# Two transformer blocks on one core: last units completed by bank, the Sqrt's table loaded before the squares, the second next split after the norm, first two units interleaved

## Chip, core and metric

The kernel runs on one core of a Trainium2 chip. The metric is the device time of one execution in microseconds (us); lower is better. Engines: TensorE (PE, with PEld for its weight loads), VectorE (DVE), ScalarE (ACT), GpSimd (POOL) and SyncE (SP), which here only issues DMAs.

## What is computed

256 tokens of width 1024, in fp32, pass through a first block (FFN, token mixer, FFN, with an RMS norm ahead of each and one behind) and a second of two layers (attention with convolution, then an expert layer). Every sublayer has the same frame:

```python
h = modulate(rms_norm(x, g), shift, scale)        # mean of squares over 1024 channels, sqrt, divide
x = x + gate * sublayer(h)                        # shift, scale, gate from c by adaptive weights
# sublayers: 0.5 * swiglu(h, w_in, w_out)         (twice, 2816 hidden)
#            token_mixer(h) ... @ mix_w_out
#            merged(attention, conv) @ w_out      (per layer)
#            peer(h): experts, sum over 16384     (per layer)
return rms_norm(x, final_g)
```

## The kernel before

**Data.** Everything is held transposed: 128 channels on the partitions, 256 tokens along them, so x is eight tiles of 128x256 (`x_t`). Weights come as 864 *units* of 128x1024 fp32 (512 KB) in the order of their use, through `ring`, four slots filled by SP: the load for a slot waits until DVE has *taken* the unit before in it. For precision each unit is split: ACT copies it to `w_hi` (`hi`, line 393), DVE subtracts to get `w_lo` (`lo`, line 731), and PE computes a product of three parts: for each of eight tiles t `w_hi` with `h_hi` and with `h_lo`, then for each t `w_lo` with `h_hi`; 24 matmuls (`product`, lines 1452 to 1467). `w_hi` and `w_lo` have two buffers each, so unit u + 2 is split once unit u is done (semaphore `weights_used`, kept by PE): that is `step(u)` on ACT and DVE, and it is written there at the point where u is used. `first` and `shared` tell when an accumulation begins; `st` and `acc` are four PSUM banks each, and `acc_t` sees `acc` as eight tiles of 256, two to a bank.

**Two kinds of unit.** An *output* unit (`tile`) gives one 128x256 tile of a result and needs all eight tiles of h. A *row* unit (`accumulate`, `kmajor`) multiplies one tile of h and adds to all eight tiles of `acc_t`. A sublayer's last product is of row units: the FFN's down-projection (lines 1501 to 1503), `mix_w_out`, `w_out`. The experts' last product (`v_unit`, lines 1848 to 1865) has tokens on the partitions: 12 matmuls of 512 columns into four banks.

**Between two sublayers** stands one chain. After the last unit DVE adds `gate * acc_t` to `x_t` tile by tile (`add_to_x`, lines 839 to 844), ACT squares each tile as it is ready (line 418), PE sums the squares over the channels with a matrix of ones (line 1473), ACT takes the Sqrt (line 420), DVE the reciprocal (line 756), and then for each tile DVE multiplies (765), ACT adds the shift and rounds to `h_hi` (426), DVE gives `h_lo` (760), and PE's first unit waits for it tile by tile (`fresh`). Each stage ends in a barrier of all engines (`stage`). After the experts the sums have first to be copied to SBUF (ACT line 717, DVE line 1341, after the whole last unit) and transposed back by PE (line 1883).

**Order.** Each engine's program is written out by hand; nothing is rearranged. Within the last unit of a sum, `step` on ACT and DVE splits the *second* unit of the next sublayer before `add_to_x` and `squares`.

## Time and profile before

| | |
|---|---|
| median of three runs | 3363.89 us (3363.59 to 3364.19) |
| the profiled execution | 3363.27 us, span 3361.6 us |
| mean granted PE clock in it | 0.941 |
| PE busy | 3070.9 us, 91% of the span, 22464 matmuls |
| PE weight loads busy | 2828.1 us (84%) |
| DVE busy | 2346.1 us (70%) |
| ACT busy | 1358.5 us (40%) |
| ring loads | 864 of 512 KB, median 3.3 us from issue to landing |

A clock of 1.00 is PE's full one, 2.4 GHz, and 0.50 the other of its two levels, 1.2 GHz. Times in the timelines are from the start of the span. A row's bracket tells how long its engine had been idle and what ended that. Where a row stands for several instructions ("x8"), its length is from the first one's start to the last one's end.

### The profile page before, as it was taken

The page shows a single profiled execution, that of the slowest core. Times are in us where ns is not written, and L with a number is a line of the kernel's source. Part 1 is how long each engine was busy: PE and PEld are TensorE (multiplying, and loading weights), DVE is VectorE, ACT ScalarE, POOL GpSimd, SP SyncE. Part 2 cuts the span into 40 slices and gives each one's busy share as a digit, 9 for nine tenths or more (in the row PEclk, how much of TensorE's full clock was granted, in tenths as well). Part 3 has the DMA queues.
Part 4 walks back from the last instruction along what each step waited for, and adds up shares of the span by engine and source line. Part 5 has one row for each costly group of instructions (what it writes and reads, how often), then busy time and mean ns, then how long its engine had stood idle before and what let it go on. Part 6 is the DMA issues. An engine that isn't in the chain of part 4 may idle for free. (4 is left out here: it accounts for less than half of the span.)

```text
span 3361.6 us, 61755 instructions
## 1 busy us (share of the span) xinstructions
PE 3070.9 (91%) x22464; PEld 2828.1 (84%) x22464; DVE 2346.1 (70%) x3735; ACT 1358.5 (40%) x1960; POOL 185.4 (6%) x204
## 2 busy tenths in 40 slices
PE   3998988889989768999999999998799999999998
PEld 2998976779979668989998878797699899988887
...
DMA packets 149585, 547.98 MB, mean 163 GB/s; under 512 B 16608, under 2 KB 16736, under 8 KB 149088
## 3 DMA queue, kind: packets, MB, share of 16 engines
...
q8 instruction: 79, 1.29, 0.2%
q14 instruction: 34, 0.28, 0.0%
HBM read 545.29 MB, written 1.05 MB: 163 GB/s over the span
## 5 line engine op out<-in xcount | busy, mean ns | idle before, releaser
L731 DVE TENSOR_TENSOR w_lo<-ring,w_hi 128x1024 fp32r<-128x1024 f32 x864 | 1087.3, 1260 | 647.1 <-ACT w_hi L393 640.4
L393 ACT ACTIVATE w_hi<-ring 128x1024 fp32r<-128x1024 f32 x864 | 910.9, 1054 | 1124.5 <-PE st L1465 935.9
L1461 PE MATMUL st<-h_hi,w_hi 128*128 128x256 f32 x4064 | 1038.5, 292 | 42.8 <-DVE h_lo L760 26.7
L1462 PE MATMUL st<-h_lo,w_hi 128*128 128x256 f32 x4064 | 1016.1, 287 | 0.0
L1461 PEld LDWEIGHTS st<-h_hi,w_hi 128*128 128x128 f32 x4064 | 795.0, 196 | 62.6 <-issue 38.4
L1462 PEld LDWEIGHTS st<-h_lo,w_hi 128*128 128x128 f32 x4064 | 795.7, 196 | 1.0
L1465 PE MATMUL st<-h_hi,w_lo 128*128 128x256 f32 x4064 | 581.5, 286 | 23.1 <-DVE w_lo L731 22.8
L1465 PEld LDWEIGHTS st<-h_hi,w_lo 128*128 128x128 f32 x4064 | 532.3, 195 | 29.5 <-DVE w_lo L731 29.5
L1856 PE MATMUL acc<-w_hi,act_hi 128*128 128x512 f32 x1024 | 322.1, 396 | 3.8 <-DVE act_lo L1278 3.8
L1856 PE MATMUL acc<-w_hi,act_lo 128*128 128x512 f32 x1024 | 316.0, 390 | 0.0
L694 ACT ACTIVATE act_hi<-arena 128x256 fp32r (+1 forms) x256 | 106.5, 417 | 438.9 <-PE acc L1862 430.8
L1862 PE MATMUL acc<-w_lo,act_hi 128*128 128x512 f32 x1024 | 274.4, 390 | 0.0
L1856 PEld LDWEIGHTS acc<-w_hi,act_lo 128*128 128x128 f32 x1024 | 192.5, 188 | 40.8
L1862 PEld LDWEIGHTS acc<-w_lo,act_hi 128*128 128x128 f32 x1024 | 192.8, 188 | 40.1
L1856 PEld LDWEIGHTS acc<-w_hi,act_hi 128*128 128x128 f32 x1024 | 189.3, 190 | 40.2 <-issue 4.1
L1278 DVE TENSOR_TENSOR act_lo<-arena,act_hi 128x256 fp32r<-128x256 f32 x256 | 108.5, 425 | 128.7 <-ACT act_hi L694 127.2
L1829 PE MATMUL st<-extra 128*128 128x64 bf16 x3072 | 193.8, 246 | 4.0 <-DVE extra L1263 4.0
L1829 PEld LDWEIGHTS st<-extra 128*128 128x128 bf16 x3072 | 171.8, 123 | 24.3 <-issue 16.4
L1461 PE MATMUL acc<-h_hi,w_hi 128*128 128x256 f32 x416 | 115.9, 310 | 54.5 <-DVE h_lo L750 26.1
L1263 DVE TENSOR_TENSOR extra<-extra,k 128x1024 bf16<-128x1024 f32 (+1 forms) x128 | 155.9, 1218 | 0.0
L1258 DVE TENSOR_TENSOR extra<-extra 128x512 bf16<-128x512 bf16 x384 | 139.4, 418 | 0.0
L1461 PEld LDWEIGHTS acc<-h_hi,w_hi 128*128 128x128 f32 x416 | 89.5, 215 | 57.8 <-DVE h_lo L750 26.7
...
## 6 DMA issues: line engine op xcount, KB each, us to landing
ring<-weights SPq DMA_DIRECT2D x864, 512.0 KB, 3.3
...
```

Of the source, the lines that this page charges most:

```text
L393: nc_a.activation(w_hi[:, u % 2, :], ring[:, u % RING, :], ACT.Copy).then_inc(hi_ready, 1)
L694: nc_a.activation(act_hi[:, n % 2, :], src, ACT.Copy).then_inc(sem("gated_hi"), 1)
L731: v.tensor_tensor(w_lo[:, u % 2, :], ring[:, u % RING, :], w_hi[:, u % 2, :], ALU.subtract)\
L1258: ins = v.tensor_tensor(hot_r[b][k], hot_r[b][0], spread(gate_parts[:, k, :], g, i, HALF), ALU.mult)
L1263: v.tensor_tensor(hot_l[g % 2], keys_t[:, 0, tokens(g, i)].unsqueeze(2).to_broadcast([P, GROUP, NKEYS]), kc("iota").unsqueeze(1).to_broadc ...
L1278: v.tensor_tensor(act_lo[:, n % 2, :], src, act_hi[:, n % 2, :], ALU.subtract) .then_inc(sem("gated_lo"), 1)
L1461: mm(dst(t), w, hi_t(t), start=start, stop=False, skip_group_check=True)
L1462: mm(dst(t), w, lo_t(t), start=False, stop=False, skip_group_check=True)
L1465: ins = mm(dst(t), w_lo[:, u % 2, t * P:(t + 1) * P], hi_t(t), start=False, stop=last and (t == DT - 1 or not shared), skip_group_check=True)
L1829: ins = mm(st[:, 2 + g % 2, :].rearrange("p (n t) -> p n t", t=GROUP)[:, :, k], hot_l[g % 2][:, k, :], hot_r[g % 2][part_][:, k // 2, :, k ...
L1856: mm(acc[:, 2 * t + half, :], act_part[:, b, t * P:(t + 1) * P], w_hi[:, u % 2, 512 * half:512 * half + 512], start=False, stop=False, ski ...
L1862: ins = mm(acc[:, 2 * t + half, :], act_hi[:, b, t * P:(t + 1) * P], w_lo[:, u % 2, 512 * half:512 * half + 512], start=False, stop=last, ...
```

## The change

Four things, at every place where one sublayer ends and the next begins:

1. The last row unit of a sum (`finish`) does its three matmuls for a tile together, and signals after each bank of two tiles (`acc_bank`; the last by `weights_used`). `add_to_x` waits by bank. The experts' last unit (`last_v_unit`) likewise completes bank by bank (`y_bank`), and the four copies wait for their own bank. `finish` and `last_v_unit` wait for `w_lo` before their first matmul.
2. ACT runs a one-column Sqrt into `spare` before the squares, so the table of that function is loaded there.
3. `step` for the last unit is left out on ACT and DVE. The second next unit is split in `norm` (`second`): on ACT ahead of the norm's tiles, on DVE behind them. For ACT the last four bodies of the FFN loop are written out.
4. PE's first two units after a norm run side by side (`first_two`): for each tile both units' products with `w_hi` and the first unit's with `w_lo`, then the second unit's eight with `w_lo`. It waits for both units' `w_hi`. The first unit is signalled as done after the 40 matmuls.

```diff
@@ ScalarE @@
             def squares(n):
+                nc_a.activation(spare[:, :], kc("eps"), ACT.Sqrt)
                 for t in range(DT):
...
-            def norm(m, shift):
+            def norm(m, shift, second=None):
+                if second is not None:
+                    hi(second)
                 for t in range(DT):
                     eng.wait_ge(sem("nh"), DT * m + t + 1)
...
-                    step(base + 5 + 3 * j, i, per)
+                    if j < FT - 2:
+                        step(base + 5 + 3 * j, i, per)
...
-                with eng.Fori(0, (FT - 2) // 4) as i:
+                with eng.Fori(0, (FT - 6) // 4) as i:
                     for j in range(4):
                         body(1 + j, i, 12)
+                for j in range(FT - 5, FT - 1):
+                    body(j)
...
-            steps(U_MIXO, 8)
+            steps(U_MIXO, 7)
...
-                eng.wait_ge(used, nth(base + 2 * NKEYS - 1))
                 for half in range(2):
+                    eng.wait_ge(sem("y_bank"), 3 * l + 2 * half + 1)
                     nc_a.activation(y_tok[:, half, :], acc[:, half, :], ACT.Copy).then_inc(sem("y_act"), 1)
@@ VectorE @@
                 if b is not None:
                     lower(DT - 2)
                     lower(DT - 1)
+                if second is not None:
+                    lo(second)
...
-            def add_to_x(gate):
+            def add_to_x(gate, n, u):
                 for t in range(DT):
+                    if t < 6:
+                        eng.wait_ge(sem("acc_bank"), 3 * n + t // 2 + 1)
+                    else:
+                        eng.wait_ge(used, nth(u))
...
-                step(base + N_FFN - 1)
-                add_to_x(half_gate[:, 8 * f:8 * f + 8])
+                add_to_x(half_gate[:, 8 * f:8 * f + 8], (0, 2)[f], base + N_FFN - 1)
...
-                eng.wait_ge(used, nth(v_base + NKEYS - 1))
                 for half in range(2):
+                    if half == 0:
+                        eng.wait_ge(sem("y_bank"), 3 * l + 2)
+                    else:
+                        eng.wait_ge(used, nth(v_base + NKEYS - 1))
@@ TensorE @@
+            def finish(u, lhs_t, rhs_t, first=False):
+                eng.wait_ge(hi_ready, nth(u))
+                eng.wait_ge(taken, u + 1)
+                for t in range(DT):
+                    w = slice(t * P, (t + 1) * P)
+                    mm(acc_t[:, t, :], w_hi[:, u % 2, w], lhs_t, start=False, stop=False, skip_group_check=True)
+                    mm(acc_t[:, t, :], w_hi[:, u % 2, w], rhs_t, start=False, stop=False, skip_group_check=True)
+                    ins = mm(acc_t[:, t, :], w_lo[:, u % 2, w], lhs_t, start=False, stop=True, skip_group_check=True)
+                    if t % 2 == 1:
+                        ins.then_inc(used if t == DT - 1 else sem("acc_bank"), 1)
+
+            def first_two(u, dsts, fresh, one_bank):
+                eng.wait_ge(hi_ready, nth(u + 1))
+                eng.wait_ge(taken, u + 1)
+                for t in range(DT):
+                    w = slice(t * P, (t + 1) * P)
+                    eng.wait_ge(sem("norm_lo"), DT * fresh + t + 1)
+                    for k in range(2):
+                        mm(dsts[k], w_hi[:, (u + k) % 2, w], h_hi[:, t, :], start=t == 0 and not (one_bank and k),
+                           stop=False, skip_group_check=True)
+                        mm(dsts[k], w_hi[:, (u + k) % 2, w], h_lo[:, t, :], start=False, stop=False,
+                           skip_group_check=True)
+                    ins = mm(dsts[0], w_lo[:, u % 2, w], h_hi[:, t, :], start=False, stop=t == DT - 1,
+                             skip_group_check=True)
+                ins.then_inc(used, 1)
+                eng.wait_ge(taken, u + 2)
+                for t in range(DT):
+                    ins = mm(dsts[1], w_lo[:, (u + 1) % 2, t * P:(t + 1) * P], h_hi[:, t, :], start=False,
+                             stop=t == DT - 1, skip_group_check=True)
+                ins.then_inc(used, 1)
...
+                def last_v_unit():
+                    u, b = base + 2 * NKEYS - 1, (NKEYS - 1) % 2
+                    eng.wait_ge(sem("gated_lo"), n_key + NKEYS)
+                    eng.wait_ge(hi_ready, nth(u))
+                    eng.wait_ge(taken, u + 1)
+                    for half in range(2):
+                        for t in range(TT):
+                            cols = slice(512 * half, 512 * half + 512)
+                            for act_part, w in ((act_hi, w_hi), (act_lo, w_hi), (act_hi, w_lo)):
+                                ins = mm(acc[:, 2 * t + half, :], act_part[:, b, t * P:(t + 1) * P], w[:, u % 2, cols],
+                                         start=False, stop=w is w_lo, skip_group_check=True)
+                            ins.then_inc(used if (half, t) == (1, 1) else sem("y_bank"), 1)
```

The other calls of `norm`, `steps`, `add_to_x` and `kmajor` change in the same way; for the very first norm there is no second split, since both units are split before it.

ACT from the last steps of the first FFN's loop to the first steps of the mixer's projection, before:

```order
L393 ACTIVATE w_hi<-ring 128x1024 [waits weights_used]
L468 REGISTER_ALU
L468 COMPARE_AND_BRANCH
L418 ACTIVATE arena<-x_t 128x256 [waits x_tile] x8
L420 ACT_TABLE_LOAD
L420 ACTIVATE extra<-st,k 128x256 [waits sumsq]
L426 ACTIVATE h_hi<-arena,mod 128x256 [waits nh,stage_done]
L426 ACTIVATE h_hi<-arena,mod 128x256 [waits nh] x7
L393 ACTIVATE w_hi<-ring 128x1024 [waits weights_used,landed0]
L393 ACTIVATE w_hi<-ring 128x1024 [waits weights_used,landed1]
```

The same place on ACT in the changed kernel:

```order
L394 ACTIVATE w_hi<-ring 128x1024 [waits weights_used,landed1]
L457 ACTIVATE act_hi<-arena 128x256 [waits act]
L394 ACTIVATE w_hi<-ring 128x1024 [waits weights_used,landed2]
L417 ACT_TABLE_LOAD
L417 ACTIVATE spare<-k 128x1
L421 ACTIVATE arena<-x_t 128x256 [waits x_tile] x8
L423 ACTIVATE extra<-st,k 128x256 [waits sumsq]
L394 ACTIVATE w_hi<-ring 128x1024 [waits weights_used,landed3,stage_done]
L431 ACTIVATE h_hi<-arena,mod 128x256 [waits nh] x8
L394 ACTIVATE w_hi<-ring 128x1024 [waits weights_used,landed0]
L394 ACTIVATE w_hi<-ring 128x1024 [waits weights_used,landed1]
```

The last `w_hi` before the squares is gone, table and one-column Sqrt stand ahead of the squares, and that `w_hi` follows the norm's Sqrt.

DVE at the same exit, from the adaptive bias to the norm's reciprocal (`nscale` is the next norm's scale), before:

```order
L812 TENSOR_TENSOR mod<-mod,par 128x40 [waits ada_mod]
L898 TENSOR_SCALAR half_gate<-mod 128x8 [waits dve_chain]
L731 TENSOR_TENSOR w_lo<-ring,w_hi 128x1024 [waits w_hi_ready,dve_chain]
L842 SCALAR_TENSOR_TENSOR x_t<-acc,half_gate,x_t 128x256 x8
L815 SCALAR_TENSOR_TENSOR nscale<-mod,par 128x8
L815 SCALAR_TENSOR_TENSOR nscale<-mod,par 128x8 [waits dve_chain]
L756 RECIPROCAL extra<-extra 128x256 [waits dve_chain,std,stage_done]
```

The same place on DVE in the changed kernel:

```order
L823 TENSOR_TENSOR mod<-mod,par 128x40 [waits ada_mod]
L913 TENSOR_SCALAR half_gate<-mod 128x8 [waits dve_chain]
L857 SCALAR_TENSOR_TENSOR x_t<-acc,half_gate,x_t 128x256 [waits acc_bank,dve_chain]
L857 SCALAR_TENSOR_TENSOR x_t<-acc,half_gate,x_t 128x256 [waits acc_bank] x5
L857 SCALAR_TENSOR_TENSOR x_t<-acc,half_gate,x_t 128x256 [waits weights_used] x2
L826 SCALAR_TENSOR_TENSOR nscale<-mod,par 128x8
L826 SCALAR_TENSOR_TENSOR nscale<-mod,par 128x8 [waits dve_chain]
L765 RECIPROCAL extra<-extra 128x256 [waits dve_chain,std,stage_done]
```

The `w_lo` between the half gate and the adds has left, and the adds wait by bank.

PE from the squares' sums to the first tiles of the projection, before:

```order
L1473 MATMUL st<-arena,k 128x256 [waits sq] x8
L1461 MATMUL st<-h_hi,w_hi 128x256 [waits norm_lo,w_hi_ready,stage_done]
L1462 MATMUL st<-h_lo,w_hi 128x256
L1461 MATMUL st<-h_hi,w_hi 128x256 [waits norm_lo]
L1462 MATMUL st<-h_lo,w_hi 128x256
L1461 MATMUL st<-h_hi,w_hi 128x256 [waits norm_lo]
L1462 MATMUL st<-h_lo,w_hi 128x256
L1461 MATMUL st<-h_hi,w_hi 128x256 [waits norm_lo]
L1462 MATMUL st<-h_lo,w_hi 128x256
L1461 MATMUL st<-h_hi,w_hi 128x256 [waits norm_lo]
```

The same place on PE in the changed kernel:

```order
L1525 MATMUL st<-arena,k 128x256 [waits sq] x8
L1508 MATMUL st<-h_hi,w_hi 128x256 [waits w_taken,norm_lo,w_hi_ready,stage_done]
L1510 MATMUL st<-h_lo,w_hi 128x256
L1508 MATMUL st<-h_hi,w_hi 128x256
L1510 MATMUL st<-h_lo,w_hi 128x256
L1512 MATMUL st<-h_hi,w_lo 128x256
L1508 MATMUL st<-h_hi,w_hi 128x256 [waits norm_lo]
L1510 MATMUL st<-h_lo,w_hi 128x256
L1508 MATMUL st<-h_hi,w_hi 128x256
L1510 MATMUL st<-h_lo,w_hi 128x256
L1512 MATMUL st<-h_hi,w_lo 128x256
L1508 MATMUL st<-h_hi,w_hi 128x256 [waits norm_lo]
```

Each tile of the norm now releases five matmuls, four with `w_hi` of two units and one with `w_lo` of the first, where it released two.

## Rows read from the trace of the kernel before

**Rows 1.** The page's groups: ScalarE's copy of a unit's weights (busy us, mean ns | idle).
```profile
L393 ACT ACTIVATE w_hi<-ring 128x1024 fp32r<-128x1024 f32 x864 | 910.9, 1054 | 1124.5 <-PE st L1465 935.9
```

**Rows 2.** Timeline, exit of the first FFN (start us, us, engine, line, operation).
```profile
281.24 0.17 DVE L898 TENSOR_SCALAR half_gate<-mod 128x8 f32<-128x8 f32 x1
281.69 1.22 DVE L731 TENSOR_TENSOR w_lo<-ring,w_hi 128x1024 fp32r<-128x1024 f32 x1 [0.27 <-ACT w_hi L393]
282.83 3.22 DVE L842 SCALAR_TENSOR_TENSOR x_t<-acc,half_gate,x_t 128x256 f32<-128x256 f32 x8
...
283.81 5.32 PE L1473 MATMUL st<-arena,k 128*128 128x256 f32 x16 [3.32 <-ACT arena L418]
...
289.16 0.47 ACT L420 ACTIVATE extra<-st,k 128x256 f32<-128x256 f32 x1 [1.36 <-PE st L1473]
```

**Rows 3.** Timeline, exit of layer 1's attention output.
```profile
2419.88 1.23 DVE L731 TENSOR_TENSOR w_lo<-ring,w_hi 128x1024 fp32r<-128x1024 f32 x1 [1.65 <-ACT w_hi L393]
...
2423.89 3.22 DVE L842 SCALAR_TENSOR_TENSOR x_t<-acc,mod,x_t 128x256 f32<-128x256 f32 x8
...
2424.87 6.56 PE L1473 MATMUL st<-arena,k 128*128 128x256 f32 x16 [3.31 <-ACT arena L418]
```

**Rows 4.** Timeline, exit of layer 0's attention output.
```profile
1240.48 6.54 PE L1473 MATMUL st<-arena,k 128*128 128x256 f32 x16 [5.41 <-ACT arena L418]
```

**Rows 5.** Timeline, exits of the experts, layer 0 and layer 1.
```profile
2170.24 1.23 DVE L731 TENSOR_TENSOR w_lo<-ring,w_hi 128x1024 fp32r<-128x1024 f32 x1 [1.25 <-ACT w_hi L393]
...
2174.10 1.28 DVE L1341 COPY arena<-acc 128x512 f32<-128x512 f32 x2
...
2174.93 2.79 PE L1883 MATMUL st<-k,arena 128*128 128x128 f32 x12 [3.16 <-DVE arena L1341]
2176.05 2.58 DVE L1344 SCALAR_TENSOR_TENSOR x_t<-st,mod,x_t 128x256 f32<-128x256 f32 x6 [0.68 <-PE st L1883]
...
2178.22 3.62 PE L1473 MATMUL st<-arena,k 128*128 128x256 f32 x16
...
3344.92 1.53 PE L1883 MATMUL st<-k,arena 128*128 128x128 f32 x12 [1.06 <-ACT arena L717]
3345.61 2.44 DVE L1344 SCALAR_TENSOR_TENSOR x_t<-st,mod,x_t 128x256 f32<-128x256 f32 x6 [0.33 <-PE st L1883]
...
3349.31 1.28 ACT L420 ACT_TABLE_LOAD   x1
3350.60 0.47 ACT L420 ACTIVATE extra<-st,k 128x256 f32<-128x256 f32 x1
```

**Rows 6.** Stretches: us, busy us (instructions) by engine, PEclk, DMA share, GB/s.
```profile
2424.87:2431.43 6.56, 6.55 (x16) 4.96 (x16) 2.24 (x6) 3.97 (x8) 0.00 (x0) 0.56 0.24 80
3346.72:3350.34 3.62, 3.62 (x18) 2.83 (x16) 2.12 (x6) 3.60 (x8) 0.00 (x0) 1.00 0.00 0
...
2174.93:2178.06 3.13, 3.13 (x15) 3.13 (x16) 2.46 (x6) 1.45 (x4) 0.00 (x0) 0.50 0.55 173
69.48:78.92 9.44, 9.44 (x49) 8.05 (x49) 5.83 (x13) 5.14 (x9) 0.00 (x0) 0.68 0.96 396
2186.06:2196.84 10.78, 10.78 (x48) 9.39 (x49) 5.83 (x13) 3.66 (x7) 0.00 (x0) 0.58 0.00 1
```

**Rows 7.** Timeline, start of the mixer's projection, up to the third unit.
```profile
293.34 0.36 PE L1461 MATMUL st<-h_hi,w_hi 128*128 128x256 f32 x1 [4.22 <-DVE h_lo L760]
...
296.68 1.27 DVE L760 SCALAR_TENSOR_TENSOR h_lo<-arena,mod,h_hi 128x256 fp32r<-128x256 f32 x3
...
298.66 1.91 PE L1465 MATMUL st<-h_hi,w_lo 128*128 128x256 f32 x8
...
302.45 1.12 PE L1465 MATMUL st<-h_hi,w_lo 128*128 128x256 f32 x8
...
303.41 0.28 PE L1461 MATMUL st<-h_hi,w_hi 128*128 128x256 f32 x1
```

**Rows 8.** DMAs of line 378, the ring's loads: issue to landing.
```profile
DMA to landing us min/median/max: 3.0/3.3/7.9
```

80 lines of the change are left out of this document (44 added, 36 removed).

## The prediction, made before the changed kernel was timed

> **What bounds the kernel now.** I read the page first: TensorE (PE) is busy for 91% of the span, so time comes back only where it stands still or runs at its low clock. I then searched the trace for such stretches. Those that the change touches lie around the norms: an *exit*, from the last unit of a sum to the Sqrt on ScalarE (ACT), and a *start*, from the first matmul after a norm to the first one of the third unit. There are seven exits (first FFN, mixer output, second FFN, and for each of two layers the attention output and the experts) and seven starts (each FFN, the mixer's projection, and each layer's projection and queries). In all of them the work is one chain, so a microsecond taken from it is one off the end.
>
> At an exit the reader is to see three things. VectorE (DVE) splits one more unit of weights before its first add to x [rows 2, 3]. PE has stood still for 3.3 us when the squares reach it, and its clock is then low: the sum of squares takes it 6.56 us at a mean clock of 0.56 [rows 3, 6], against 3.62 us at 1.00 at the last exit, where it had stood still for 1.06 [rows 5, 6]. And the Sqrt comes 4.7 to 7.6 us after the first add, as that clock decides. At a start PE waits for each tile of the norm, which DVE delivers every 0.79 us at first, with the last one 4.6 us after PE's first matmul [rows 7]; its clock is low again for most of the first two units [rows 6].
>
> **Exits: the first add comes earlier.** DVE no longer splits the second next unit (1.22 us [rows 2]) there, and doesn't wait for its ACT copy (1.05 us [rows 1]).
> - First FFN: half_gate ends at 281.41; the split begins at 281.69 and the adds at 282.83 [rows 2]. Now they follow at once, at 281.48: 1.35 earlier. PE's last unit ends at 280.49, so here the banks bring nothing: DVE is the late one. The second FFN is alike, 1.35.
> - Attention output, layer 1: the split before ends at 2421.11, the adds begin at 2423.89 [rows 3]. The first bank is complete some 0.8 us into the unit that ends at 2421.56, so DVE can add at 2421.04: 2.85. The mixer output has the same order: 2.85.
> - Attention output, layer 0: DVE is behind with the adaptive weights, with PE idle for 5.41 us before the squares [rows 4]. Only the split goes: 1.15. The last unit now waits for its own split before its first matmul and ends some 1.6 us later than before, still 1.6 us before the first add, so that is hidden.
> - Experts, layer 0: the copies began at 2174.10, behind the second split, and the first add came 1.95 us later; now they begin at 2171.47, where the first split ends [rows 5]. That gives 2.65. Two copies take DVE 1.28 us, and the first transposes now run beside the second copy: first add at 2172.95 instead of 2176.05, 3.1. Layer 1 has no split there; one copy of DVE's (0.64) and one of ACT's move under the last unit: I take 0.75.
>
> Sum of the shifts: 2 x 1.35 + 2 x 2.85 + 1.15 + 3.1 + 0.75 = 13.4 us.
>
> **Exits: squares at the full clock.** With the adds earlier, PE stands still for about 0.5 us at the mixer, at layer 1's attention and at layer 0's experts, where it was 3.3, 3.3 and 3.2 [rows 3, 5]. At the last exit 1.06 us left the clock at 1.00 [rows 5, 6]. At full clock the sum of squares ends 4.73 us after the first add (3345.61 to 3350.34 [rows 5, 6]); I take 4.8 to the Sqrt. Before it was 6.33 (first FFN), 6.43 (second), 6.42 (mixer), 7.57 (layer 1's attention), 5.8 (layer 0's experts), 5.0 (last) [rows 2, 3, 5]. Gains: 1.5 + 1.6 + 1.6 + 2.8 + 1.0 + 0.2 = 8.7. At the FFN exits PE still idles 2.0 us, between the 1.06 that kept the clock and the 3.3 that lost it; I lean to kept, and take off 0.7 for doubt. At layer 0's attention the idle time falls from 5.41 to 2.6; its squares took 6.54 us [rows 4], 2.9 more than at the full clock, and at even chances that is 1.4. Sum 9.4 us.
>
> **The table load** moves ahead of the squares, into ACT's waiting. Only in the last exit does it end last: squares' matmuls end at 3350.34, the load at 3350.59 [rows 5]; those 0.2 us are in the 5.0 above. But once the clock is kept, the load would end last everywhere (the eight Squares are done 3.7 us after the first add, plus 1.28 = 4.95), so the move protects 0.2 us per exit. The Trainium skill ("ScalarE: Activation LUTs", What ACT_TABLE_LOAD costs) counts a drain of 1.38 us with each switch, 2.66 us in all; by that the move would be worth 1.6 us at the last exit. The row disagrees: the load begins at 3349.31 and the Sqrt at 3350.60, 1.29 us later.
>
> **Starts: two units side by side.** The second unit's split moves: on ACT behind the Sqrt (1.05 us, while DVE takes the reciprocal, and PE's first matmul is 4.2 us away), on DVE behind the norm's last tile. PE gets five matmuls per tile where it had two, then eight for the second unit's low part. A matmul is issued every 0.214 us at the low clock (1.91 - 0.41 over 7) and every 0.12 at the full one (1.12 - 0.28 over 7) [rows 7]. Five at the low clock are 1.07 us per tile of 0.79: PE waits no more. The 48 matmuls took 9.44, 10.07, 10.21, 10.56, 10.60, 10.78 and 10.62 us (first, and longest, in [rows 6]; the second 293.34 to 303.41 in [rows 7]), 72.3 together. All low would be 10.3, all full is bounded by the tiles: 4.6 + 1.35 for the split + 0.96 = 6.9.
>
> When does the clock rise? From the mean clock, 0.68 over 9.44 us is low for 6.0 us, 0.58 over 10.78 is low for 9.1 [rows 6]. PE had stopped waiting for tiles about 4 us in. So it rose 2.0 to 5.1 us after PE began to run without gaps. Now that begins with the first matmul; I take 3.5. Then 16 matmuls low and 24 full end at 6.4 us, the last eight at 7.4. The third unit's ACT copy waits for the first unit to be done, which is now signalled after 40 matmuls: 6.4 + 1.05 + 0.2 = 7.65. With 5.1: 8.25. I take 7.95, so 10.33 - 7.95 = 2.4 per start, 16.6 in all.
>
> **Sum.** 13.4 + 9.4 + 16.6 = 39.4 us. The profiled run took 3363.3 (span 3361.6), 0.6 below the median of three, 3363.9: 3363.9 - 39.4 = 3324.5 us.
>
> Costed at nothing: the new order inside the last units (as many matmuls as before, hidden by DVE, which is later), and the four bodies written out on ACT, which issue the same work.
>
> **Rivals.**
> 1. *The clock gives nothing.* It falls at exits and rises at starts when it did before. For: no row shows PE idle for 2 us and what follows. Against: 3.62 us for the squares at the last exit [rows 6]. Then the exits give 13.4 + 0.2, and the starts only the gaps: about 1.0 each less 0.2 for the third unit's copy, 6: 3363.9 - 19.6 = 3344.
> 2. *Half of it.* FFN exits and layer 0's attention stay low (less 1.5 + 1.6 - 0.7 + 1.4 = 3.8), and the rise at the starts comes at 5.1 (less 2): 3330.5. With starts at 2.0 and exits all kept it would be 3320.
> 3. *Transposes don't hold the clock.* At the experts' exits 16 transposes come before the squares. The row: in the 3.13 us from 2174.93 PE did only transposes at clock 0.50, and the squares right behind them took 3.62 us, the full-clock time [rows 5, 6]; so they count as work. If they didn't, the squares there would cost 2.8 more each: 3330. The Trainium skill ("TensorE: Matmul & The Clock Gate", Part 4: PE-mode transpose) says that the full clock "doesn't engage" for transposes; by that rule it would be this case, and the trace disagrees.
> 4. *Slower: refills come late.* Taking the second unit's split 12 us later frees its ring slot 12 us later, and the unit four further on is loaded into it. That load is issued about 5.9 us after the first matmul and its unit is copied at 7.95 + 2 x 2.9 = 13.7: 7.8 us of slack. A load lands in 3.3 us, at most 7.9 [rows 8]. It costs from 7.8 on, and eats the gain where it takes some 5.6 us more at all seven starts, 13.4 us; at 15 us it gives 3363.9 + 11 = 3375. Nothing in the rows comes near.
> 5. *The change doesn't do what it says*: were DVE late at every exit, as at the FFNs, banks would bring nothing there; they are counted at 1 to 2 us in all, so 3326, inside the forecast.
>
> **Chances.** Forecast (3318 to 3329, both clock effects, with rival 5) 0.65; rivals 2 and 3 (3329 to 3336) 0.17; rival 1 and what lies between (3336 to 3350) 0.12; more than forecast 0.02; no difference 0.02; slower 0.02. The range 3317 to 3340 leaves out less than 2 in 10. What a measurement can tell from no change is 0.2%, 6.7 us: faster 0.96, same 0.02, slower 0.02.
>
> **What would show it.** In the changed profile: first add about 281.5 less what was gained before; squares in 3.6 us at clock 1.00 at the mixer, both experts and layer 1's attention; Sqrt 4.8 us after the first add; table loads ahead of the squares; third unit 7.5 to 8.3 us after the first matmul, its copy on ACT ending just before. Wrong if the clock column stays at 0.50 to 0.56 in the squares, if a unit waits on DMA behind a start, or if the Sqrt comes 6 us after the first add.

## The result, and the profile after

The changed kernel takes 3323.2 us (median of four runs, 3320.4 to 3326.9), the kernel before 3363.7 (four runs, 3361.9 to 3364.2): a ratio of 0.9882, with a 95% interval of 0.9867 to 0.9897. The forecast was 3324.5, in a range of 3317 to 3340. The profiled execution of the changed kernel is its slowest, 3326.9 us with a span of 3325.2, and stands 36.4 us below the profiled one of before. So the traces have to explain 36.4; the median run is 3.7 us better still, and where that comes from is one of the questions below.

| profiled execution | before | after |
|---|---|---|
| span, us | 3361.6 | 3325.2 |
| PE busy, us | 3070.9 | 3048.9 |
| mean granted clock | 0.941 | 0.942 |
| the seven exits (last unit's end to the Sqrt), us | 64.9 | 39.1 |
| the seven starts (Sqrt to the third unit's first matmul), us | 101.5 | 88.0 |
| all the rest, us | 3195.1 | 3198.1 |

(Between the second FFN's exit and the start behind it lies the first block's final norm; it is counted with "the rest".) The mean clock over the whole span is all but the same. What changed is where its low stretches lie, and the page's clock row doesn't show that: one has to ask for the stretches. By the clock record the exits and starts have the low clock for 48 us where they had it for 89. But ahead of the first Sqrt it is low for 31 us instead of 14, which cost 1.1 us, and on the way to layer 1's attention output for 72 instead of 58.

**The exits.** The timeline of the changed kernel at the first FFN, which answers to [rows 2] (start us, us, engine, line, operation, and in brackets how long the engine had been idle and what ended that):

```profile
281.07 0.17 DVE L913 TENSOR_SCALAR half_gate<-mod 128x8 f32<-128x8 f32 x1
...
281.28 3.23 DVE L857 SCALAR_TENSOR_TENSOR x_t<-acc,half_gate,x_t 128x256 f32<-128x256 f32 x8
...
282.26 3.72 PE L1525 MATMUL st<-arena,k 128*128 128x256 f32 x16 [0.56 <-ACT arena L421]
...
286.02 0.47 ACT L423 ACTIVATE extra<-st,k 128x256 f32<-128x256 f32 x1 [1.07 <-PE st L1525]
```

The adds follow the half gate at once, where a copy's wait and a split lay between them, and the sum of squares takes 3.72 us where it took 5.32. Layer 1's attention output, for [rows 3], with the table load and the last split ahead of the adds:

```profile
2392.88 1.28 ACT L417 ACT_TABLE_LOAD   x1
2392.89 1.23 DVE L740 TENSOR_TENSOR w_lo<-ring,w_hi 128x1024 fp32r<-128x1024 f32 x1 [1.65 <-ACT w_hi L394]
...
2394.03 3.22 DVE L857 SCALAR_TENSOR_TENSOR x_t<-acc,mod,x_t 128x256 f32<-128x256 f32 x8
...
2395.01 3.72 PE L1525 MATMUL st<-arena,k 128*128 128x256 f32 x16 [0.44 <-ACT arena L421]
...
2398.77 0.47 ACT L423 ACTIVATE extra<-st,k 128x256 f32<-128x256 f32 x1 [1.07 <-PE st L1525]
```

The adds start right behind the one split that is left, PE stands still for 0.44 us where it was 3.31, and the Sqrt comes 4.74 us after the first add, where it was 7.58. The table has long been there. The second FFN and layer 0's attention output [rows 4] are the two exits whose squares still ran partly at the low clock:

```profile
942.28 3.23 DVE L857 SCALAR_TENSOR_TENSOR x_t<-acc,half_gate,x_t 128x256 f32<-128x256 f32 x8
...
943.27 5.41 PE L1525 MATMUL st<-arena,k 128*128 128x256 f32 x16 [1.95 <-ACT arena L421]
```

```profile
1224.81 5.21 PE L1525 MATMUL st<-arena,k 128*128 128x256 f32 x16 [2.56 <-ACT arena L421]
```

And the experts' exit of layer 0, for [rows 5]: the copies run under the last unit (L1935), and behind ACT's last copy stands the table load. The transposes follow the unit with no gap to speak of, and the adds come 0.74 us after its end, where it was 4.28.

```profile
2147.57 1.49 DVE L1360 COPY arena<-acc 128x512 f32<-128x512 f32 x2
...
2147.94 0.39 PE L1935 MATMUL acc<-w_lo,act_hi 128*128 128x512 f32 x1
...
2148.30 1.28 ACT L417 ACT_TABLE_LOAD   x1
...
2149.07 2.44 DVE L1363 SCALAR_TENSOR_TENSOR x_t<-st,mod,x_t 128x256 f32<-128x256 f32 x6
...
2153.92 0.47 ACT L423 ACTIVATE extra<-st,k 128x256 f32<-128x256 f32 x1 [1.18 <-PE st L1525]
```

**The starts.** The mixer's projection, for [rows 7], from the first matmul to the third unit:

```profile
290.20 0.55 PE L1508 MATMUL st<-h_hi,w_hi 128*128 128x256 f32 x1 [4.22 <-DVE h_lo L769]
...
293.54 1.27 DVE L769 SCALAR_TENSOR_TENSOR h_lo<-arena,mod,h_hi 128x256 fp32r<-128x256 f32 x3
...
297.62 1.12 PE L1517 MATMUL st<-h_hi,w_lo 128*128 128x256 f32 x8
...
297.88 2.02 ACT L394 ACTIVATE w_hi<-ring 128x1024 fp32r<-128x1024 f32 x2 [3.72 <-PE st L1512]
...
299.00 0.38 PE L1478 MATMUL st<-h_hi,w_hi 128*128 128x256 f32 x1 [0.25 <-ACT w_hi L394]
```

The third unit comes 8.80 us after the first matmul, where it was 10.07, and waits 0.25 us for its copy on ACT, as forecast. Between these rows PE has no gap; what makes the start long is its clock. The stretches of the changed kernel (us, busy us and instructions of PE, PEld, DVE, ACT, POOL, then the granted clock, DMA share, GB/s), for [rows 6]: the squares of the first FFN, the second FFN, layer 0's and layer 1's attention, the transposes at layer 0's experts, and three starts (first FFN, mixer, layer 1's queries):

```profile
282.26:285.99 3.73, 3.72 (x16) 2.91 (x16) 2.48 (x8) 2.69 (x7) 0.00 (x0) 1.00 0.00 0
943.27:948.67 5.40, 5.40 (x16) 4.09 (x16) 2.24 (x6) 2.69 (x7) 0.00 (x0) 0.68 0.00 0
1224.81:1230.01 5.20, 5.20 (x16) 4.04 (x16) 2.51 (x8) 2.69 (x7) 0.00 (x0) 0.71 0.00 0
2395.01:2398.74 3.73, 3.72 (x16) 2.91 (x16) 2.24 (x6) 2.69 (x7) 0.00 (x0) 1.00 0.44 141
2148.90:2150.17 1.27, 1.27 (x14) 1.21 (x12) 1.26 (x4) 1.26 (x4) 0.00 (x0) 1.00 0.93 345
70.59:78.32 7.73, 7.48 (x49) 7.27 (x49) 4.62 (x13) 3.65 (x8) 0.00 (x0) 0.78 0.99 410
290.20:299.00 8.80, 8.54 (x49) 8.34 (x49) 5.83 (x14) 3.67 (x8) 0.00 (x0) 0.67 0.17 58
2402.95:2411.78 8.83, 8.57 (x48) 8.37 (x49) 5.76 (x14) 3.66 (x8) 0.00 (x0) 0.67 0.18 61
```

Squares at 1.00 take 3.72 us and at 0.68 to 0.71 they take 5.2 to 5.4. A start in which the clock is low for 3.4 us (0.44 of 7.73) lasts 7.7 us, one in which it is low for 5.8 us lasts 8.8.

Place by place, from the traces (us; the rise is when the clock goes to 1.00 after the first matmul, from the clock record; a start stands in the row of the exit ahead of it, and for the second FFN behind the final norm):

| | exit before | after | start before | after | clock's rise, before | after |
|---|---|---|---|---|---|---|
| first norm | | | 13.63 | 11.91 | 6.0 | 3.6 |
| first FFN | 8.67 | 4.31 | 14.25 | 12.98 | 7.4 | 5.8 |
| mixer output | 8.75 | 4.20 | 14.38 | 12.78 | 7.7 | 5.3 |
| second FFN | 8.77 | 7.39 | 14.75 | 12.79 | 8.5 | 5.4 |
| attention, layer 0 | 11.98 | 7.80 | 14.78 | 11.92 | 8.6 | 3.9 |
| experts, layer 0 | 10.11 | 5.59 | 14.96 | 12.62 | 9.1 | 5.0 |
| attention, layer 1 | 9.90 | 4.20 | 14.80 | 13.01 | 8.7 | 5.9 |
| experts, layer 1 | 6.74 | 5.58 | | | | |
| sum | 64.9 | 39.1 | 101.5 | 88.0 | | |

### The profile page after: what moved, and what is told of

Same layout as the page of the kernel before. It is cut to its first block and busy times, and to the rows that moved or that the text cites. A ratio compares the mean times of both kernels' runs of the same rounds, so it can differ in the third digit from the quotient of the medians.

```text
span 3325.2 us, 61743 instructions
## 1 busy us (share of the span) xinstructions
PE 3048.9 (92%) x22464; PEld 2815.6 (85%) x22464; DVE 2345.2 (71%) x3735; ACT 1359.3 (41%) x1969; POOL 185.1 (6%) x204
## 3 DMA queue, kind: packets, MB, share of 16 engines
q8 instruction: 79, 1.29, 0.2%
## 5 line engine op out<-in xcount | busy, mean ns | idle before, releaser
L1478 PE MATMUL st<-h_hi,w_hi 128*128 128x256 f32 x3952 | 989.0, 288 | 17.8 <-DVEq L323 11.4
L1479 PE MATMUL st<-h_lo,w_hi 128*128 128x256 f32 x3952 | 972.8, 284 | 0.0
L1478 PEld LDWEIGHTS st<-h_hi,w_hi 128*128 128x128 f32 x3952 | 762.3, 193 | 26.5 <-DVEq L323 12.4
L1479 PEld LDWEIGHTS st<-h_lo,w_hi 128*128 128x128 f32 x3952 | 761.1, 193 | 1.0
L1482 PE MATMUL st<-h_hi,w_lo 128*128 128x256 f32 x3952 | 560.9, 285 | 23.2 <-DVE w_lo L740 22.8
L1482 PEld LDWEIGHTS st<-h_hi,w_lo 128*128 128x128 f32 x3952 | 512.5, 193 | 29.5 <-DVE w_lo L740 29.4
(284 smaller groups left out, 3300.6 us busy)
## 6 DMA issues: line engine op xcount, KB each, us to landing
arena<-smallw ACTq DMA_DIRECT2D x1, 320.0 KB, 10.4
```

What stands on the lines that cost most here:

```text
L1478: mm(dst(t), w, hi_t(t), start=start, stop=False, skip_group_check=True)
L1479: mm(dst(t), w, lo_t(t), start=False, stop=False, skip_group_check=True)
L1482: ins = mm(dst(t), w_lo[:, u % 2, t * P:(t + 1) * P], hi_t(t), start=False, stop=last and (t == DT - 1 or not shared), skip_group_check=True)
```

## The experiments

The theory is the prediction's: three gains in three places (earlier adds, squares at the full clock, starts without gaps), with almost nothing for banks and table. Its rivals were that the clock gives nothing, and that parts only change places. Each kernel is compared with the kernel before as it ran beside it, 3363.6 to 3364.4 us. The sums by place are those of the one profiled execution of each:

| kernel | median, us | ratio to before, 95% | exits | starts | rest |
|---|---|---|---|---|---|
| before | 3363.6 to 3364.4 | | 64.9 | 101.5 | 3195.1 |
| changed | 3323.2 | 0.9882 (0.9867 to 0.9897) | 39.1 | 88.0 | 3198.1 |
| starts alone | 3344.0 | 0.9942 (0.9928 to 0.9955) | 62.9 | 86.6 | 3192.4 |
| changed without starts | 3332.6 | 0.9907 (0.9892 to 0.9922) | 40.6 | 101.7 | 3187.9 |
| changed without table move | 3323.2 | 0.9879 (0.9864 to 0.9894) | 41.1 | 86.2 | 3191.4 |
| changed without banks | 3325.1 | 0.9883 (0.9868 to 0.9898) | 45.9 | 86.8 | 3192.5 |
| moved split alone | 3333.9 | 0.9909 (0.9894 to 0.9925) | 46.1 | 101.5 | 3184.7 |
| changed, clock held | 3313.1 | 0.9848 (0.9834 to 0.9861) | 37.2 | 80.9 | 3193.4 |
| changed, late adaptive work | 3310.4 | 0.9841 (0.9827 to 0.9854) | 30.3 | 85.1 | 3190.2 |
| both of these | 3302.2 | 0.9816 (0.9802 to 0.9829) | 30.3 | 80.4 | 3186.9 |
| both, GpSimd's loads behind | 3300.6 | 0.9813 (0.9799 to 0.9826) | 30.4 | 79.7 | 3186.2 |
| before, 8 products more | 3360.9 | 0.9990 (0.9981 to 1.0000) | 63.6 | 102.6 | 3189.1 |
| before, 16 products more | 3361.6 | 0.9991 (0.9981 to 1.0000) | 65.0 | 101.9 | 3193.0 |
| before, 24 products more | 3361.3 | 0.9988 (0.9979 to 0.9998) | 65.0 | 101.8 | 3193.7 |

### The starts alone

```diff
-                up(base, 0, fresh=(0, 2)[f])
+                first_two(base, [st[:, 0, 0:T], st[:, 2, 0:T]], (0, 2)[f], False)
...
+                    if p == 0:
+                        first_two(base, [st[:, 0, 0:T], st[:, 0, T:2 * T]], fresh, True)
                     for k in range(2):
-                        tile(st[:, p % 4, k * T:(k + 1) * T], base + 2 * p + k,
-                             fresh=fresh if (p, k) == (0, 0) else None)
+                        if p > 0:
+                            tile(st[:, p % 4, k * T:(k + 1) * T], base + 2 * p + k)
```

> The kernel before with the fourth part alone: PE's first two units after a norm side by side, all else as it was (the second unit is still split ahead of the adds). Theory (the starts gain by themselves, since PE has work for each tile and its clock rises sooner): the seven starts took 72.3 us before and 58.7 in the changed kernel's trace, so 13.6 us less, 3363.7 - 13.6 = 3350; 3347 if each start ends at the 7.95 us of the forecast. Rival (the clock gives nothing, only the gaps between tiles close, 6 us in all): 3358. Rival (the starts are short only because the exits ahead of them are): starts of 10 us and more again, about 3360. In the trace the exits are as before, with squares of 5.3 to 6.6 us.

Measured: 3344.0, 20.4 us less, more than any of the three. The starts themselves give 15.0 us (101.5 to 86.6), so they gain by themselves, with the old long exits ahead of them; both rivals are out. The other 5 us lie elsewhere: 2.0 in the exits and 2.7 in the rest, where this kernel computes just what the one before does. Two of its stretches, the squares at layer 0's experts and the start behind them:

```profile
2161.77:2165.39 3.62, 3.62 (x18) 2.84 (x16) 2.12 (x6) 3.60 (x8) 0.00 (x0) 1.00 0.08 31
2169.83:2178.56 8.73, 8.48 (x48) 8.27 (x48) 4.62 (x13) 3.72 (x8) 0.00 (x0) 0.68 0.00 0
```

The start is 8.73 us at a mean clock of 0.68, where it was 10.78 at 0.58 [rows 6]. The squares were at 1.00 before too; what got shorter in that exit are the transposes ahead of them, 1.50 us for twelve where it was 2.79 [rows 5], behind the same 3.16 us of idle PE.

### The changed kernel without the starts

The first unit takes the tiles alone again, two matmuls for each, and the second unit follows (the diff is the one above, undone).

> The changed kernel without its fourth part: the first unit takes the tiles alone, two matmuls a tile, and the second follows; split, banks and table stay as changed. Theory (parts add up): 3323.2 + 13.6 = 3337, up to 3340. Rival (a clock that is kept through the squares also shortens the old starts, so that the parts overlap): 3333 or less, with starts below 9.5 us. Rival (the second unit now waits for its late split, so that the moved split needs the new order): 3343 and more, with PE idle on the low part of the second unit.

Measured: 3332.6, lower than the theory's 3337 and at the first rival's 3333. But that rival's mark, starts below 9.5 us, isn't there: the starts take 101.7 us in all as in the kernel before, and PE waits nowhere for the moved split. So the exits keep their gain alone (40.6), the starts lose theirs alone, and the 4 us of surprise are in the rest, 3187.9 us, 10 us less than in the changed kernel's trace; 9.5 of them lie in one stretch of the mixer, on which the last experiment is. Its two FFN exits and the start of layer 1's queries:

```profile
283.58:288.99 5.41, 5.41 (x16) 4.09 (x16) 2.47 (x8) 2.69 (x7) 0.00 (x0) 0.68 0.00 0
940.68:944.40 3.72, 3.72 (x16) 2.91 (x16) 2.24 (x6) 2.69 (x7) 0.00 (x0) 1.00 0.00 0
2403.83:2413.94 10.11, 9.88 (x48) 8.52 (x49) 6.97 (x14) 3.61 (x7) 0.00 (x0) 0.66 0.18 53
```

Here the first FFN lost the clock and the second kept it, each after PE had stood still for 1.94 to 1.95 us; in the changed kernel the first had kept it (after 0.56 us) and the second lost it.

### The changed kernel without the table move

```diff
             def squares(n):
-                nc_a.activation(spare[:, :], kc("eps"), ACT.Sqrt)
                 for t in range(DT):
```

> The changed kernel without the one-column Sqrt ahead of the squares, so that the table is loaded behind the last square again. Theory (a load costs its own 1.28 us and ends 4.95 us after the first add, where the sum of squares ends at 4.74 at the full clock): 0.2 us at each of the five exits whose squares ran at the full clock, nothing at the two at the low clock: 1.0 us, 3324.2, and the Sqrt 4.95 to 5.0 us after the first add. Rival, by the Trainium skill ("ScalarE: Activation LUTs", What ACT_TABLE_LOAD costs: 2.66 us with the drain): 1.6 us at each of the five, 8 us, 3331. Rival (the early load was in the way of something): 3322 or less.

Measured: 3323.2, the same. At layer 1's attention output:

```profile
2386.91 3.22 DVE L856 SCALAR_TENSOR_TENSOR x_t<-acc,mod,x_t 128x256 f32<-128x256 f32 x8
...
2390.60 1.28 ACT L422 ACT_TABLE_LOAD   x1
2391.89 0.47 ACT L422 ACTIVATE extra<-st,k 128x256 f32<-128x256 f32 x1
```

The Sqrt comes 4.98 us after the first add where it was 4.74, and 1.29 us after the load began. By the rows the move is worth 0.24, 0.14, 0.24 and 0.04 us at four exits whose squares ran at 1.00, 0.7 us in all; at the mixer output there is no load in either kernel, since the Sqrt's table is there already. That is too little for the medians to show. The Trainium skill ("ScalarE: Activation LUTs", What ACT_TABLE_LOAD costs) adds a drain of 1.38 us to each load; no row here shows one.

### The changed kernel without banks

```diff
                 for t in range(DT):
-                    if t < 6:
-                        eng.wait_ge(sem("acc_bank"), 3 * n + t // 2 + 1)
-                    else:
+                    if t == 0:
                         eng.wait_ge(used, nth(u))
...
-                finish(base + N_FFN - 1, act_hi[:, b, :], act_lo[:, b, :])
+                accumulate(base + N_FFN - 1, (FT - 1) % 2, last=True)
...
-                for n in range(NKEYS - 4, NKEYS - 1):
+                for n in range(NKEYS - 4, NKEYS):
                     v_unit(n)
-                last_v_unit()
```

> The changed kernel without its first part: last units in the old order of matmuls, and adds and copies wait for the whole unit. Theory (banks give little, since the moved split is what brings the adds forward): the first add comes 0.6 us later at the mixer output and at layer 1's attention, the experts' copies 1.0 to 1.5 later at both layers, nothing at the FFNs and at layer 0's attention, where VectorE is late anyway: 3 to 4 us, 3327; PE stands still for 1.0 to 1.1 us ahead of the squares and the clock is kept, 3.7 us for the squares. Rival (with whole units PE stands still long enough to lose the clock at the mixer and at layer 1's attention): 1.7 to 2.8 us more at each, 3331 and more. Rival (banks are nothing at all, since a last unit that waits for its own split is paid for): 3323.

Measured: 3325.1, 1.9 us more. The traces give 0.6 us at the mixer output, 0.6 at layer 1's attention, 1.2 at each of the experts' exits, 3.6 in all; at the second FFN nothing changes, and at the first and at layer 0's attention the unit ends earlier by about what the exit is longer. Layer 1's attention:

```profile
2394.56 3.72 PE L1507 MATMUL st<-arena,k 128*128 128x256 f32 x16 [1.02 <-ACT arena L421]
...
2398.32 0.47 ACT L423 ACTIVATE extra<-st,k 128x256 f32<-128x256 f32 x1 [1.07 <-PE st L1507]
```

PE stands still for 1.02 us and the squares take 3.72 all the same: whole units don't cost the clock. The first rival is out; between the theory and "nothing" the medians can't tell, the rows say 3.6. The banks without the moved split weren't run.

### The moved split alone

The kernel before with the third part only: `norm` takes `second`, the last `step` ahead of each exit is gone on ACT and DVE.

> The kernel before with the third part alone: the second next unit is split behind the norm; whole last units, old starts, table behind the squares. Theory (the moved split is what shortens the exits, banks and table add next to nothing): without the first part the exits took 45.9 us where they were 64.9 in the kernel before, and 0.2 us more at four of them for the table, so 18 us less: 3364.4 - 18 = 3346, 3342 to 3350 as the stretches between norms fall. Rival (the split only changes places: what leaves the exits comes back at the second unit of each start): 3360, with starts of 12 us. Rival (banks and moved split only work together): 3355 and exits of 55 us.

Measured: 3333.9, 12 us lower than the theory. The exits fall by 18.8 us to 46.1, as the theory had them, and the starts stay at 101.5, so nothing comes back at the second unit; nor are the exits near the 55 us of a split that needs the banks. Both rivals are out. Another 10.4 are in the rest, 3184.7, and nearly all of them in one stretch, from the third projection unit to the mixer's last unit, which the split doesn't touch: 414.15 us where it was 423.84. That was a new question, and the last experiment is on it.

### The clock held through the norm

```diff
+            def fill(u, n, dst):
+                w = w_hi[:, u % 2, :]
+                eng.wait_ge(hi_ready, nth(u))
+                for _ in range(n):
+                    mm(dst, w[:, 0:P], w[:, 0:T], start=True, stop=True, skip_group_check=True)
+
             def first_two(u, dsts, fresh, one_bank):
+                spare_bank = st[:, 1, 0:T]
+                fill(u, 16, spare_bank)
+                eng.wait_ge(sem("nh"), DT * fresh + 1)
+                fill(u, 5, spare_bank)
+                eng.wait_ge(sem("norm_hi"), DT * fresh + 1)
+                fill(u, 4, spare_bank)
...
             stage(eng, ST["ffn1"])
+            fill(U_L2 + O_QK, 20, st[:, 1, 0:T])
             squares(4)
```

> The changed kernel, and PE kept at work between the squares and the norm's first tile with 25 products that nobody reads (16 behind the barrier, 5 behind the norm's first tile, 4 behind its rounding), and 20 ahead of the final norm's squares. Theory (the starts are long because the clock falls while PE waits for the norm, 4.2 us): the clock stays at 1.00 behind exits that kept it, the third unit comes 6.9 us after the first matmul, as tiles and split then decide, where it was 8.4 on average: 7 x 1.5 = 10.5 us less, and 2 to 3 less in the final norm: 3310. Rival (the clock falls all the same, for instance in the 1 us ahead of the barrier): the 25 products take 5.4 us in a wait of 3.6, and each start comes up to 1 us later: 3328. Rival (a start at the full clock is bound by the tiles, as long as before): 3321.

Measured: 3313.1, 10.1 us below the changed kernel. From the Sqrt to the third unit behind the mixer output and behind layer 0's experts, and the final norm:

```profile
723.31:734.63 11.32, 10.64 (x77) 9.32 (x77) 9.33 (x19) 6.48 (x12) 2.18 (x4) 1.00 0.56 194
...
2143.48:2154.80 11.32, 10.46 (x74) 9.22 (x74) 9.34 (x19) 6.48 (x12) 0.00 (x0) 1.00 0.04 6
...
942.08:949.15 7.07, 6.36 (x36) 5.33 (x36) 5.09 (x10) 3.86 (x10) 2.08 (x4) 1.00 0.69 259
```

All run at 1.00: six starts take 11.3 us from the Sqrt to the third unit, where they were 11.9 to 13.0. The one behind the final norm takes 12.97, where it was 12.79. There the barrier behind the Sqrt opens late, PE stands still for 2.29 us instead of 0.60, the clock falls, and the 25 products take 4.70 us:

```profile
951.42 1.75 DVE L765 RECIPROCAL extra<-extra 128x256 f32<-128x256 f32 x1 [3.65 <-POOLq L323]
```

What ended that wait is GpSimd's queue at the barrier (line 323): it had been issuing four loads of adaptive weights from 942.88 on. I come back to it. The final norm takes 7.1 us where it was 10.2. That is 7.1 us in the starts and 3.1 in the final norm, 10.2 together, as the median has it. (The two traces differ by 13.7: another 1.9 lie in the exits, chiefly the second FFN's, which kept the clock this time, and 1.6 elsewhere.) The third unit of those six starts comes 6.7 to 7.1 us after the first matmul, near the 6.9 that the prediction worked out from the tiles and the split; 48 matmuls at its 0.12 us would take 5.8.

### Late adaptive work

```diff
-                take_block(q0 + 4, st[:, 2:4, :])
-                add_bias(q0, q0 + 5)
+                add_bias(q0, q0 + 4)
                 link(v.tensor_scalar(half_gate[:, 8 * f:8 * f + 8], gate1(2 * f), 0.5, None, ALU.mult))
+                for r in range(2):
+                    take(q0 + 4, r, quarter(st[:, 2:4, :], r ^ 2), upto=r | 1)
                 add_to_x(half_gate[:, 8 * f:8 * f + 8], (0, 2)[f], base + N_FFN - 1)
+                for r in range(2, 4):
+                    take(q0 + 4, r, quarter(st[:, 2:4, :], r ^ 2), upto=r | 1)
+                add_bias(q0 + 4, q0 + 5)
...
-                            for m in range(3 * k // 4, 3 * (k + 1) // 4):
+                            for m in [] if k in (14, 15) else [11] if k == 16 else range(3 * k // 4, 3 * (k + 1) // 4):
...
                     scale2_of(0, 1)
+                    mac(Q_OUT + 1, 2, part[:, (Q_OUT + 1) % 2, :])
```

> The changed kernel with VectorE's adaptive work taken out of three exits: at the FFNs two of the last four reductions, with their bias, stand behind the adds to x (their sums lie in another bank), at layer 0's attention the last two multiply-adds. Theory (these exits are bound by VectorE, and PE's standing still for 1.95 and 2.56 us is what may cost the clock): the Sqrt comes 4.3 us after the last unit instead of 5.7 to 7.4 at the FFNs and 7.8 at layer 0's attention: 1.5 + 3.1 + 3.5 = 8 us less, 0.4 given back at each FFN where the reductions end behind the Sqrt: 3315.5. Rival (the reductions are late for the reciprocal by more than they were for the adds): 3323 and more, with the reciprocal starting 2 us behind the barrier. Rival (the clock is lost in these exits whatever the gap): 3319.

Measured: 3310.4, 12.8 us below the changed kernel, 5 more than expected. The second FFN's exit:

```profile
933.83 3.22 DVE L857 SCALAR_TENSOR_TENSOR x_t<-acc,half_gate,x_t 128x256 f32<-128x256 f32 x8
...
934.88 3.65 PE L1530 MATMUL st<-arena,k 128*128 128x256 f32 x16
...
938.57 0.47 ACT L423 ACTIVATE extra<-st,k 128x256 f32<-128x256 f32 x1 [1.07 <-PE st L1530]
...
939.23 1.75 DVE L765 RECIPROCAL extra<-extra 128x256 f32<-128x256 f32 x1 [0.21 <-ACTq L323]
```

The adds now run under the last unit, PE goes from it to the squares without a gap, and the reciprocal follows the Sqrt as it did: the two late reductions end in time. The exits are 3.5, 3.5 and 3.7 us at the two FFNs and at layer 0's attention, where they were 4.3, 7.4 and 7.8: 8.7 us. All seven exits' squares run at 1.00. The 5 us more than expected can't be placed with certainty: the traces differ by 19.5 us, and beside those 8.7 they have 2.9 in the starts, where the clock rose earlier, and 4.9 in the mixer's stretch, which this edit doesn't touch.

### Both

> Both of the last two edits. Theory (they act in different places): 3323.2 - 13 - 7.5 = 3302.5, exits of 33 us in all and starts of 77 (Sqrt to third unit) where they are 39 and 88. Rival (a clock held in one place is lost in the stretches between, so that they don't add up): 3308 or more.

Measured: 3302.2, as the theory had it, 21.0 us below the changed kernel and 62 below the one before (0.9816). The exits are shorter than it said (30.3 us for 33) and the starts longer (80.4 for 77). In its trace neither an exit nor a start has any time at the low clock (before: 27 and 61 us of it). One wait is left of the kernel with the clock held: behind the final norm PE, ACT and DVE stand at the barrier for GpSimd, which issues its four loads between the two barriers there and is now the last to arrive:

```profile
933.67 2.08 POOL L1393 DMA_DIRECT2D arena<-ada_weights  x4 [26.53 <-ACTq L323]
```

```profile
941.79 1.75 DVE L765 RECIPROCAL extra<-extra 128x256 f32<-128x256 f32 x1 [3.14 <-POOLq L323]
```

The barrier opens 8.1 us after the first of these issues, in the kernel with the clock held 8.5; in the kernel before and in the changed one the final norm was too long for that to show.

### The loads behind the barrier

```diff
             stage(eng, ST["ffn1"])
-            first_loads(8 * Q_PROJ)
             stage(eng, ST["final1"])
+            first_loads(8 * Q_PROJ)
```

> The fastest kernel so far (clock held and late adaptive work), and GpSimd's four loads of adaptive weights, which stood between the two barriers around the final norm, moved behind the second. In the trace of the kernel with both edits the second of these barriers opens 1.7 us after the Sqrt where the others open 0.6 after it, and the engines' idle time there is ended by GpSimd, 8.1 us after its first issue. Theory (the shortened norm has made that queue the last to arrive): the start behind the final norm takes 11.3 us from the Sqrt to the third unit, as the others, not 12.45; 1.1 us less, 3301. That is under what the medians tell apart; the trace decides. Rival (another engine is as late, or it was chance): 12 us and more again. Rival (the loads now come too late for VectorE's first multiply-adds in the projection): the stretch up to layer 0's attention output, 251.9 us, gets longer by more than 2, 3304.

Measured: 3300.6, too near to 3302.2 to be told from it by the medians, but the trace shows the place:

```profile
942.68 1.75 DVE L765 RECIPROCAL extra<-extra 128x256 f32<-128x256 f32 x1 [1.99 <-ACTq L323]
```

The reciprocal starts 0.58 us after the Sqrt (942.10), released by ACT, and the start takes 11.32 us, 12.45 before this edit (five of the other six take the same, the mixer's projection 11.8 in this run). The stretch up to layer 0's attention output is 249.9 us, no longer than the 251.9 it was. Both rivals are out. This is the fastest kernel of the study, 63 us below the kernel before and 22.6 below the changed one.

### Where the mixer's stretch comes from

Three runs put products that nobody reads into the middle of the mixer's projection, where PE has work without a gap: they do nothing but shift all that follows.

```diff
                 for p in range(n):
+                    if p == 4 and base == U_MIX:
+                        for _ in range(8):
+                            mm(acc[:, 1, 0:T], h_hi[:, 0, 0:P], h_hi[:, 0, :], start=True, stop=True)
```

> The kernel before with 8 products more that nobody reads, in the mixer's projection (behind its eighth unit), where PE works without a gap at 1.00 for another 120 us: they move all that follows by 0.95 us. Theory (in the mixer's core PE stands still often, and how much of it falls to the low clock hangs on when its idle times come, so that kernels that reach it at another moment get another sum): the stretch from the third projection unit to the mixer's last one, 423.8 us before and 414.1 in the two kernels with old starts and moved split, changes by more than 0.95, and in at least one of the three shifts by 3 us or more: between 3355 and 3368. Rival (those 9.7 us belong to the moved split itself): 3364.4 + 1.0 = 3365.4, and 424.8 us for the stretch.

> The same with 16 products, 1.9 us. Theory: another sum of the stretch than in the kernel before, by 3 us or more up or down in at least one of the three; 3356 to 3370. Rival: 3366.3, and 425.7 us for the stretch.

> The same with 24 products, 2.9 us. Theory: as above, 3356 to 3371. Rival: 3367.3, and 426.7 us for the stretch.

Measured: 3360.9, 3361.6 and 3361.3, in ten runs each, from 3355.8 to 3363.7; with 1 to 3 us of work added the kernel is some 3 us faster, at the edge of what the interval resolves (for 8 and 16 products it reaches 1.0000). The traced execution with 8 products, 3356.9, is one of the two fastest of its ten. The stretch from the third projection unit to the mixer's last one, in the kernel before, the changed one, the one with the moved split alone, and the one with 8 products more:

```profile
303.41:727.25 423.84, 378.48 (x2654) 345.36 (x2652) 217.81 (x324) 141.76 (x206) 46.11 (x16) 0.86 0.26 88
```

```profile
299.00:722.62 423.62, 378.84 (x2652) 346.72 (x2652) 219.41 (x327) 141.71 (x208) 46.13 (x16) 0.85 0.26 88
```

```profile
304.00:718.15 414.15, 368.45 (x2654) 338.51 (x2652) 217.55 (x324) 141.77 (x206) 46.08 (x16) 0.88 0.27 90
```

```profile
304.02:721.08 417.06, 373.49 (x2662) 343.26 (x2660) 217.76 (x324) 141.71 (x206) 46.14 (x16) 0.87 0.27 89
```

The rival's 424.8 became 417.1 with 8 products; with 16 and 24 it is 420.6 where the rival had 425.7 and 426.7. So these microseconds don't belong to the moved split, and the changed kernel shows the same: it has the moved split and needs 423.6 us. Over all fourteen traces the stretch is 414.1 to 423.8 us long and the clock in it is low for 96 to 123 us, and the two go together: 96 with 414.1, 102 with 416.3, 109 with 418.8 to 420.6, 116 to 123 with 422.4 to 423.8. The microseconds are gained where the low clock falls on fewer busy ones; two pieces of the stretch show it, around the pooling and at the heads' sums, first before, then with the moved split alone:

```profile
451.00:489.30 38.30, 27.70 (x170) 26.13 (x168) 14.84 (x14) 10.96 (x17) 0.00 (x0) 0.72 0.23 78
646.40:656.60 10.20, 6.51 (x16) 1.97 (x16) 1.74 (x1) 1.75 (x2) 0.00 (x0) 0.67 0.00 0
```

```profile
450.10:484.50 34.40, 23.81 (x170) 22.55 (x168) 14.76 (x14) 10.96 (x17) 0.00 (x0) 0.83 0.27 87
641.30:648.60 7.30, 3.60 (x16) 1.33 (x16) 1.74 (x1) 1.75 (x2) 0.00 (x0) 1.00 0.00 0
```

The same 16 matmuls take PE 6.51 us at 0.67 and 3.60 at 1.00. What exactly has to be at which moment stays open: the shifts didn't bring the 414.1 of the two kernels with the moved split and old starts.

This is also why the medians of the parts don't add up: starts alone (20.4 us) and split alone (30.4) make 50.8, and the whole change gave 40.6. By place they nearly do: exits 2.0 and 18.8 (all together 25.8, with 3.6 for the banks and 0.7 for the table), starts 15.0 and nothing (13.5). The surplus is in the rest, 2.7 and 10.4 less than before, where the changed kernel's trace has 3.0 more.

## Why the prediction was right, point by point

**Earlier adds, 13.4 us.** Right, and a little small. Measured from the half gate the FFNs gain 1.38 each (forecast 1.35), measured from the last unit's end the mixer output and layer 1's attention gain 2.87 each (2.85). Layer 0's experts gain 3.5 (3.1), layer 1's 1.1 (0.75), and layer 0's attention 1.9, measured from the third projection unit (1.15). Together 15.0. That the last unit there now ends later was seen: it took 0.9 us more (forecast 1.6), hidden behind VectorE, with 2.56 us of idle PE left (2.6).

**Squares at the full clock, 9.4 us.** 8.5 measured, from the first add to the Sqrt. Five exits have 4.74 to 4.94 us (forecast 4.8). The FFNs were "lean to kept": one kept it and one lost it, and the step "between the 1.06 that kept the clock and the 3.3 that lost it" was too simple. With 1.94 to 1.95 us of idle PE ahead of an FFN's squares the clock was kept in five exits of these kernels and lost in five. In the changed kernel's own trace the first FFN kept it with 0.56 us of idle time, because its last unit ran late (its sums ahead had a low clock). At layer 0's attention the even chance fell on low: 2.56 us of idle PE lost the clock in four kernels of four.

**The table.** Right in size and sense: 1.28 us, no drain, 0.24 us where it ends last. But it is nothing that the time shows, and at the mixer output there is no load at all, which the timeline tells and I had not looked for.

**Starts, 16.6 us.** 13.5 in the profiled run. The order of things was right: no gaps, the ACT copy ends last, 0.25 us. The step that was mis-sized is "I take 3.5" for the clock's rise, out of a range of 2.0 to 5.1: it rose 3.6 to 5.9 us after the first matmul, 5.0 on average, and in the kernel with the starts alone 4.6 (15.0 us gained). From 3.5 to 5.1 the forecast's own working adds 0.6 us to a start, 7.65 to 8.25. Carried on, it gives 8.2 to 8.55 for rises at 5.0 to 5.9; those starts took 8.4 to 8.8, so another 0.2 to 0.3 was missed in the sum of matmuls and copy.

**The sum.** 15.0 + 8.5 + 13.5 = 37.0, and 0.6 less for all else gives the trace's 36.4. In that "all else" are moves of one to four microseconds with both signs that the prediction didn't have: 1.1 lost ahead of the first Sqrt (its squares took 4.75 us where they took 3.78), 3.6 won on the way to layer 0's experts' exit, 3.3 lost on the way to layer 1's attention. Each goes with the low clock there: 31 us of it where it was 14, 10 where it was 20, 72 where it was 58. The median run is 3.7 us better than the profiled one. I can't say where, since only one run has a trace; the starts and the mixer's stretch differ by as much from kernel to kernel. That the median lies 1.3 us from the forecast is partly luck: the adds were 1.6 too small, the squares 0.9 and the starts 3.1 too large, which makes 37.0 instead of 39.4, and the median run happened to be better than the profiled one by more than that difference.

**The signs.** Squares at 1.00 (3.70 to 3.72 us, 3.6 forecast) and the Sqrt 4.74 to 4.94 us after the first add are there at the mixer output, both experts' and layer 1's attention. But one sign of being wrong came too: at the second FFN and at layer 0's attention the Sqrt comes 6.4 and 6.2 us after the first add. The forecast had kept some doubt about the FFNs and even chances at layer 0's attention. And its range for the Sqrt before, 4.7 to 7.6 us after the first add, should begin at 5.0: 4.7 is where the squares' matmuls end [rows 5].

**The rivals.** *The clock gives nothing*: out; squares at 1.00 took 3.72 us, and the held clock alone gave another 10. *Half of it* (3330.5) is in good part what the profiled run did: layer 0's attention and one of the two FFNs at the low clock, rises at 5.0 on average. With 3326.9 that run lies between it and the forecast. *Transposes don't hold the clock*: out. In the changed kernel PE goes from the last unit over 16 transposes to the squares, and the stretch with the transposes is at 1.00, as are the squares behind. That alone proves little, since the transposes take under 2 us and idle times of 1.02 us kept the clock too; the row that decides is the one of before [rows 6], where 3.13 us of nothing but transposes began at 0.50 and the squares right behind ran at 1.00. By the Trainium skill ("TensorE: Matmul & The Clock Gate", Part 4: PE-mode transpose) the full clock would not have engaged, and the trace disagrees. *Refills come late*: out; the ring's loads still land after 3.0 to 7.9 us, 3.3 in the middle [rows 8], and the second FFN's body takes 201.7 us from the third unit on as against 201.6 before. *Banks bring nothing*: 3.6 us by the rows, against 1 to 2 counted. The sign was never in doubt: the starts alone and the moved split alone were each faster than the kernel before by more than 0.5%.
